# Three ends of layers rewritten: the last two steps by token half, the root table loaded ahead, shorter norms, and the projection in four PSUM bank pairs

## What is computed

```
def rms_norm(x, g):
    y = xf * rsqrt(mean(xf * xf, axis=-1) + 1e-6);  return y * g

mix  = token_mixer(rms_norm(h, g_mix_pre), ...)          # ends in y @ w_out      "out2"
h    = h + rms_norm(mix, g_mix_post)
ff   = conv_ffn(rms_norm(h, g_ffn_pre), ...)             # w_up: "ffn2", w_down: "down2"
h    = h + rms_norm(ff, g_ffn_post)
e    = p @ w_ple_proj                                    # 256 -> 2048            "proj"
gate = sigmoid(rms_norm(h, g_ple_in) @ w_ple_gate)       # 2048 -> 2048           "ple"
h    = h + rms_norm(e * gate, g_ple_post)                # the output
```

## Time and profile before

| | us |
|---|---|
| median of 3 runs | 2517.32 (2517.01 to 2519.24) |
| the profiled execution, its own time | 2519.18 |
| its span | 2517.4 |
| TensorE matmuls busy | 2472.1 (98%), 11947 instructions |
| VectorE busy | 1463.8 (58%), 1747 |
| ScalarE busy | 1245.5 (49%), 1596 |
| GpSimd busy | 44.9 (2%), 103 |
| mean granted clock of TensorE | 0.994 of 2.4 GHz |

### The profile page before, as it was taken

The page is one execution under the profiler, slowest core; times in us unless marked ns, Lnnn a source line. Parts: engine busy times, 40 slices in busy tenths (PEclk is TensorE's granted clock), DMA queues, the critical chain, the costliest instruction groups (busy, mean ns, idle before and its releaser), DMA issues.

```text
span 2517.4 us, 32623 instructions
## 1 busy us (share of the span) xinstructions
PE 2472.1 (98%) x11947; PEld 2065.4 (82%) x11947; DVE 1463.8 (58%) x1747; ACT 1245.5 (49%) x1596; POOL 44.9 (2%) x103
## 2 busy tenths in 40 slices
PE   8999999999999999999999999989999999999997
PEld 6888878888888888888888888878888888888876
DVE  5479665545454454446567566566666666544465
ACT  4357744444444444444654355455555565444453
POOL 2300000000000000000000000000000000000000
PEclk9999999999999999999999999999999999999999
DMA  7553445666666665555655455645656656655543
GB/s 247 175 139 112 135 146 184 189 192 190 185 191 186 190 195 200 189 192 175 170 173 144 143 151 180 192 146 175 198 178 190 183 183 190 203 192 193 194 164 133
DMA packets 234754, 446.27 MB, mean 177 GB/s; under 512 B 14288, under 2 KB 31012, under 8 KB 234144
## 3 DMA queue, kind: packets, MB, share of 16 engines
q1 hardware_dynamic: 231920, 434.83, 56.2%
q0 software_dynamic: 2736, 10.10, 1.3%
HBM read 442.78 MB, written 2.10 MB: 177 GB/s over the span
## 4 chain that ended last, share of the span: by engine, by line
PE 95%; DVE 3%; ACT 1%; issue 1%; DMA 0%; SPq 0%; DVEq 0%; ACTq 0%
PE pg L2092 27%; PE pg L2094 26%; PE pg L2093 26%; PE pg L2131 3%; PE pg L2132 3%; PE pg L2133 3%; PE pt L2707 1%; DVE wlo L1285 1%; PE pt L2547 1%; PE pt L2143 1%; PE pt L2251 1%; PE pt L2316 1%; PE pt L2342 1%; PE pt L2329 0%; DVE H L1391 0%
## 5 line engine op out<-in xcount | busy, mean ns | idle before, releaser
L1285 DVE TENSOR_TENSOR wlo<-raw,whi 128x1024 fp32r<-128x1024 f32 (+3 forms) x844 | 1005.2, 1197 | 984.9 <-ACT whi L647 983.3
L647 ACT ACTIVATE whi<-raw 128x1024 fp32r<-128x1024 f32 (+3 forms) x844 | 872.5, 1036 | 1185.7 <-PE pg L2094 1067.2
L2092 PE MATMUL pg<-whi,AH 128*128 128x512 f32 (+1 forms) x1920 | 748.5, 390 | 6.0 <-DVE AL L1402 4.4
L2094 PE MATMUL pg<-whi,AL 128*128 128x512 f32 (+1 forms) x1920 | 742.0, 386 | 0.0
L2093 PE MATMUL pg<-wlo,AH 128*128 128x512 f32 (+1 forms) x1920 | 741.4, 386 | 0.0
L2092 PEld LDWEIGHTS pg<-whi,AH 128*128 128x128 f32 x1920 | 361.4, 188 | 77.9 <-DVE AL L1402 5.3
L2094 PEld LDWEIGHTS pg<-whi,AL 128*128 128x128 f32 x1920 | 361.1, 188 | 73.4
L2093 PEld LDWEIGHTS pg<-wlo,AH 128*128 128x128 f32 x1920 | 361.6, 188 | 70.6
L2092 PE MATMUL pg<-whi,FH 128*128 128x512 f32 x704 | 274.5, 390 | 0.0
L2094 PE MATMUL pg<-whi,FL 128*128 128x512 f32 x704 | 274.0, 389 | 0.0
L2093 PE MATMUL pg<-wlo,FH 128*128 128x512 f32 x704 | 273.9, 389 | 0.0
(11 more groups left out here) (452 smaller groups left out, 2013.6 us busy)
## 6 DMA issues: line engine op xcount, KB each, us to landing
raw<-w_up SPq DMA_DIRECT2D x264, 512.0 KB, 3.8
raw<-w_down SPq DMA_DIRECT2D x176, 512.0 KB, 3.6
raw<-w_in SPq DMA_DIRECT2D x152, 512.0 KB, 3.6
raw<-w_gate SPq DMA_DIRECT2D x88, 512.0 KB, 3.6
raw<-w_out SPq DMA_DIRECT2D x64, 512.0 KB, 3.6
raw<-w_ple_gate SPq DMA_DIRECT2D x32, 512.0 KB, 3.8
raw<-w_in SPq DMA_DIRECT2D x32, 388.0 KB, 3.3
raw<-w_in SPq DMA_DIRECT2D x16, 280.0 KB, 3.0
```

Of the source, the lines that this page charges most:

```text
L647: A(whi[:, n % RING, 0:w], raw[:, n % RING, 0:w], ACT.Copy).then_inc(hi_ready, 1)
L1285: V.tensor_tensor(wlo[:, n % RING, 0:w], raw[:, n % RING, 0:w], whi[:, n % RING, 0:w].bitcast(F32), ALU.subtract).then_inc(lo_ready, 1)
L2092: mm(o, xh, wh, start=first and k == 0, stop=False)
L2094: ins = mm(o, xl, wh, start=False, stop=last and k == SK - 1)
```

## The change

1. **Last two steps by token half** (`last_two` on TensorE, in `out2`, `down2` and `ple`). Before, each of the last two steps did both halves. Now both steps' products of half 0 come first (`half_used`), then those of half 1 (`step_used` by 2). ScalarE reads half 0 while half 1 is computed.
2. **Root table ahead.** ScalarE's and VectorE's loops end two splits earlier (30 of 32, 86 of 88). `root_table` comes after them and before the last squares; the two splits left come after the root.
3. **After the sums.** VectorE takes the root's result and goes on to `H` at once; the product with the gain of the last chunk (`evac(3)`) comes later: in `out2` inside `ffn2`'s first chunk (`last_add`), in `down2` after two splits. The first quarter of `H` is added in two pieces of 256 columns (`post_first`), each turned and cut alone (`turn_part`, `prep_part`). The turns of the other quarters come at steps 1, 3 and 5.
4. **Norms.** `inverse` folds the last two small steps into one and the -0.5 into the first (5 or 6 small instructions instead of 6 or 7); for the three post-norms the first one comes before the wait for the root. The norms of `in1` and `ffn1` leave two steps between their squares and their root; in `ffn2` and `ple` ScalarE squares both halves.
5. **Projection.** Its four chunks get four pairs of banks (`e_bank`: `pg`, `pt` 0 and 1, `pt` 2 and 3, `pg`); ScalarE alone copies them out (`e_copy`). The first turn of `ple` comes before the projection's last chunk.
6. **Tail.** Gate, product and squares go by token half; `e_gained` writes to `FO` and follows each gate at once.

The core of the diff:

```
+            def last_two(n, b, kt0, hi, lo):
+                for t in range(NT):
+                    o = pg[:, b + t, :]
+                    for i in range(2):
+                        if t == 0:
+                            pe.wait_ge(lo_ready, n + i + 1)
+                        for k in range(SK):
+                            ...
+                            mm(o, xh, wh, start=False, stop=False)
+                            mm(o, xh, wl, start=False, stop=False)
+                            ins = mm(o, xl, wh, start=False, stop=i == 1 and k == SK - 1)
+                    if t == 0:
+                        ins.then_inc(half_used, 1)
+                    else:
+                        ins.then_inc(step_used, 2)

+            def e_bank(c, t):
+                b = 2 * ((G["proj"]["C"] + c) % 2)
+                return (pg[:, b + t, :], pt[:, t, :], pt[:, 2 + t, :], pg[:, b + t, :])[c]

             def rstd(i, n, before=False):
+                if i not in (5, 7, 9):
+                    dve.wait_ge(root, i + 1)
+                link(V.tensor_scalar(SM[:, 6:8], SM[:, 0:2], -0.5 / n, -0.5 * EPS, ALU.mult, ALU.add))
                 dve.wait_ge(root, i + 1)
-                link(V.tensor_scalar(SM[:, 6:8], SM[:, 0:2], 1.0 / n, EPS, ALU.mult, ALU.add))
-                refine(SM[:, 8:10], SM[:, 6:8], SM[:, 2:4], SM[:, 10:12])
-                ...
-                V.tensor_tensor(SM[:, 4:6], SM[:, 8:10], SM[:, 10:12], ALU.mult).then_inc(rstd_ready, 1)
+                inverse(SM[:, 4:6], SM[:, 6:8], SM[:, 2:4], SM[:, 8:10], SM[:, 10:12], SM[:, 4:6] if before else None)\
+                    .then_inc(rstd_ready, 1)

 VectorE, end of out2:
+            post_sums(8)
             rstd(5, D)
-            dve.wait_ge(gained, 4)
-            post_add(MIX, 0)
+            dve.wait_ge(gained, 3)
+            post_first(MIX)
+            prep_part(5, f2_cols, AH, AL, 0)
             post_add(MIX, 1)
-            f2_in(0)()
+            prep_part(5, f2_cols, AH, AL, 1)
+            split(F2["N"] + 2)
+            f2_in(1)()
+            split(F2["N"] + 3)
             post_add(MIX, 2)
-            f2_in(1)()
-            post_add(MIX, 3)
+            def last_add():
+                evac(3, 0, G["out2"]["N"] + 32)
+                dve.wait_ge(gained, 4)
+                post_add(MIX, 3)
             ffn(F2, ...
-                {1: f2_in(2), 2: f2_in(3), 4: norm_ffn2})
+                {2: f2_in(2), 3: last_add, 4: f2_in(3), 7: lambda: rstd(6, D)})

 VectorE, between down2 and ple:
-            proj(0)
+            post_sums(16)
             rstd(7, D)
+            dve.wait_ge(gained, 7)
+            split(p0["N"] + 2)
+            post_first(FO)
+            split(p0["N"] + 3)
+            evac(3, 0, G["down2"]["end"])
+            post_add(FO, 1)
+            split(g["N"])
+            prep_part(6, ple_cols, OH2, OL2, 0)
+            prep_part(6, ple_cols, OH2, OL2, 1)
+            split(g["N"] + 1)
+            post_add(FO, 2)
+            ple_in(1)()
+            split(g["N"] + 2)
             dve.wait_ge(gained, 8)
-            ...
             post_add(FO, 3)
+            split(g["N"] + 3)

 TensorE, projection and ple:
+            proj(0)
+            proj(1)
+            proj(2)
+            pe.wait_ge(e_out, 4)
+            pe.wait_ge(h_first, 2)
+            turn_part(6, 0)
+            pe.wait_ge(h_block, 5)
+            turn_part(6, 1)
+            proj(3)
```

More of the change, by code:

```diff
@@ L1201, in _ @@
             evac = evac_squares(G["out2"], 0)
-            for i in range(32):
+            for i in range(30):
                 between.get(i, no)()
@@ L1619, in side @@
                         dve.wait_ge(x_landed[c], 16)
[L1620 removed]
+                    squares(0, H[:, 1, :], XN[:, 1, :])
+                if n == 5:
+                    rstd(0, D)
                 if n == 10:
@@ L2024, in _ @@
+            for i in range(4 * S_ - 2):
+                hooks.get(i, no)()
+                split(g["N"] + RING + i)
+                if i % S_ == S_ - 1:
+                    evac(i // S_, 0, g["N"] + i + 1)
             if upto < 18: return
-            def proj(c):
-                evac_copy(E, G["proj"])(c, 0, G["proj"]["N"] + c + 1)
-                split(G["ple"]["N"] + c)
-            proj(0)
+            p0, g = G["proj"], G["ple"]
+            ple_cols = lambda k: V_GPLE + k
+            ple_in = lambda c: lambda: prep(6, ple_cols, OH2, OL2, c)
@@ L2047, in _ @@
-            ple_in(1)()
-            between = {(0, 1): ple_in(2), (0, 2): ple_in(3), (0, 4): norm_ple}
-            def e_gained(c):
-                dve.wait_ge(gain_landed, 64)
-                dve.wait_ge(sq_ready, 16 + 2 * c + 2)
-                for t in range(NT):
-                    x = E[:, t, c * CW:(c + 1) * CW]
-                    ins = V.tensor_tensor(x, x, GP[:, c * CW:(c + 1) * CW], ALU.mult)
-                ins.then_inc(gained, 1)
-            g = G["ple"]
+            dve.wait_ge(gained, 7)
@@ L2562, in f2_pair @@
                 else:
-                    first(5, h_tiles, lambda q: pe.wait_ge(h_block, q + 1), AH, AL, F2)
+                    chunk(F2, 0, before=lambda j: post_turns(5, AH, AL, 0, j, 1))
                 chunk(F2, 2 * c + 1, 0, 4, dc, dn)
@@ L2584, in down @@
                 for c in range(1, 4):
-                    chunk(g, c, hi=FH, lo=FL, before=before(c))
+                    two = g is G["down2"] and c == 3
+                    chunk(g, c, 0, g["S"] - 2 if two else g["S"], hi=FH, lo=FL, before=before(c))
+                if two:
+                    last_two(g["end"] - 2, 2 * ((g["C"] + 3) % 2), FKT - 2 * SK, FH, FL)
             def fox_q():
@@ L2800, in _ @@
             out2(2, 0, 8, 16)
-            out2(3, 0, 8, 24)
+            out2(3, 0, 6, 24)
+            last_two(G["out2"]["end"] - 2, 2 * ((G["out2"]["C"] + 3) % 2), 2 * SK, OHG, OLG)
             if upto < 17: return
```

280 lines of the change are left out of this document (196 added, 84 removed).

## The result

| us | median | executions |
|---|---|---|
| before, four executions beside it | 2517.39 | 2517.01 to 2519.24 |
| after | 2503.64 | 2502.72 to 2508.06 |
| predicted | 2500.3 | range 2496.8 to 2506.5 |

The ratio is 0.9947 (95% interval 0.993 to 0.9965): 13.8 us faster. The profiled execution of after is the slowest of its four: 2508.06, span 2506.3, mean granted clock 0.994; the others have 0.996 and 0.997.

The account below looks back on a forecast made before the run. Matmuls fill 98% of the span, so gains come only where TensorE waits or runs at its low clock. Terms 1.6 + 0.4 + 2.5 + 10.2 + 2.3 = 17.0 us gave 2500.3 us, range 2496.8 to 2506.5.

Parts of the forecast that it names:

- Start of in1: At in1's start, the 1.45 us wait for AL at 33.80 goes, with the slower first matmul: 1.6 us less.
- Start of in2: At in2's start, two waits for wlo each lose one small norm step of 0.2 us: 0.4 us less.
- End of out2: From out2's end into ffn2, a shorter chain to the first add, clock low for 6.8 us: 2.5 us less.
- down2, proj, ple: From the projection to ple's first chunk, 36 matmuls cover the norm, one 0.9 us wait, full clock: 10.2 us less.
- Rival (a): VectorE becomes the bound between down2 and ple, wait 2.5 us and clock falls: 5 us less gain, 2505.3; chance 0.17.
- Tail: Behind the last matmul, half 0's gate and squares go under matmuls, products go ahead: 2.3 us less.
- (b): out2 brings only its worst, 0.9 us, and the starts of in1 and in2 half of theirs: 2502.9; chance 0.10.
- (c): The clock stays full at out2: 2498.1; chance 0.07.
- (d): ScalarE loads the root's table again behind the half's squares, 1.3 us at out2, hidden at down2: 2501.6; chance 0.03.
- rival (e): Slower through low clock behind four short waits: 19 us lost makes it even, a fifth stretch gives 2522; chance 0.03.
- the four waits that the change makes: Short TensorE waits expected in the changed kernel: 3.1, 1.2 and 0.9 us at out2, 0.9 in ple.
- the last line of the sum: The median was put 1.9 us below the profiled execution's 2502.2, as in the kernel before: 2500.3.

Follow-up runs that it names:

- again: The changed kernel run once more with no edit, for a second profile: median 2505.74 us, ratio 0.995.
- before_again: The kernel before the change run once more, unchanged, for a second profile: median 2517.85 us.
- fill_level2: The changed kernel with five useless matmuls (1.13 us) ahead of level 2 of the HGRN sums, in TensorE's 1.41 us wait for Z: ratio 0.9942.
- in1_norm_as_before: The changed kernel with in1's norm as before, root and small steps right behind the squares: median 2503.68 us.
- fill_out2: The changed kernel with useless matmuls in TensorE's idle time behind out2, 13 ahead of ffn2's first turn and 4 behind it: median 2506.27 us.

## Why the prediction was right, step by step

Against the table, before to changed kernel:

- **Start of in1, -1.6.** "To XD" went from 338.9 to 337.2 (mean of eleven profiles with the edit): -1.7. Right, and so is the wait that went.
- **Start of in2, -0.4.** "XD to Z" without the low clock 987.1 to 986.7: -0.4. Its waits are 0.79 and 0.36 where they were 0.96 and 0.57.
- **End of out2, -2.5.** 752.9 to 750.0 in the first profile, 750.3 to 751.3 in the other five that leave this stretch alone, -1.5 to -2.9. The prediction's own terms add up to 2.6. First turn after 3.17 (3.1 predicted), waits 1.0 (1.2) and 0.66 (0.9), half adds 0.42 (0.40). The clock was low for 6.8 us (6.8), but that hit is partly luck: the term was read from one stretch of 6.8 us behind another wait, and it measured 10.2 us in `again`.
- **down2, proj, ple, -10.2.** 112.6 to 102.5, -10.1, against the second profile of before -8.7. The one wait is 0.65 (0.9). The eight transposes come without a wait, no chunk's end waits, the clock is full. Rival (a) is out. But "the clock falls as it did behind 2.6", its price, is no rule: in `before_again` the clock stayed full behind the same wait.
- **Tail, -2.3.** 15.5 to 13.2 (the four terms add up to 2.4), with the table load on the path (2494.22, 1.28 us) and the eight adds of 5.39 us as in the earlier trace rows.

Rivals (b), (c) and (d) are out for the same reasons: `out2` brought 1.5 at least, the clock was low there, and no second load came. The times alone could not tell: (b) stands at 2502.9 and (a) at 2505.3, on both sides of the first median, 2503.64, and beside the second, 2505.74. The stretches do.

The five terms sum to 17.0, and the same stretches of the profiles to 14.6 at the least and 17.4 at the most. The median gave 13.8, then 12.1. So the time lies in the range, but two steps between the sum and the time were wrong, and both concern the low clock.

The first is the one by which I dismissed rival (e): "1.45 us at 33.80 left the clock alone". I looked for new low stretches behind the four waits that the change makes, and there the sum's one at `out2` is all there is. Another came behind a wait that the change doesn't touch but moves: the one for `Z` ended 2.4 us earlier in `again` than in the kernel before, and 1.1 later in after, where 3.2 us had been lost at 337. It cost 3.2 us in both profiles of the changed kernel, and the one at 337 another 3.2 in one of them. Against the predicted span of 2500.4, `again` has 2504.2 (3.2 for `Z`, the rest mostly at `out2`) and after 2506.3 (twice 3.2, less 0.5). `fill_level2`, with neither of the two, has 2500.4, the predicted span. It and `in1_norm_as_before` show the stretch at `Z` from two sides, by filling the wait and by moving it.

The second is the last line of the sum: "the same difference gives 2500.3". The 1.9 us between the profiled execution and the median were taken over from the kernel before. There `before_again`'s profile, 1.7 us shorter at 2517.46, shows what most of it was: one low stretch less behind `down2`, 1.4 us. Behind `down2` the changed kernel has no low stretch, so no run shows such a difference in it; four of the executions of `fill_level2` lie at 2502.3 to 2502.5, where the prediction had 2502.2 for the profiled one.

Of the 3.3 us between 2500.3 and 2503.64, up to 1.9 are thus this step and the rest low stretches, which by the mean clocks came in some executions and not in others. How often, and at which moments, stays open. The mechanism was right in each place; that the median came within 3.3 us of the forecast and not 5.4, as `again`'s did, is luck.

## What to carry to other kernels

Where matmuls fill 98% of the span, put work that needs no result under the serial end of a layer: 24 matmuls in spare banks were worth 7 us here, 4.85 of waiting and 2.3 of low clock. Count as the price of a wait of TensorE not only its length but the low clock that may follow, 3.2 us behind 1.4, and expect that a gain early in the program moves every later wait to another moment. A wait that left the clock alone in one profile, or made it fall, is no proof for the next. So compare stretches between fixed instructions of the two traces, not the totals. Where TensorE must idle for 1 us or more, a few matmuls into a bank that is free anyway kept the clock full at two places here (`fill_level2`, `fill_out2`), in the profiles; with one place filled the median need not follow, since other short waits are left.

## What the runs showed of the hardware

- The granted clock fell (from 2.4 to 1.2 GHz) behind waits of 0.82 and 1.41 us in some profiles and not in others, with the same instructions in front and behind. With the wait of 1.41 us moved by 1.3 us (one profile) it stayed full, and so it did with 1.13 us of the wait filled with matmuls (two profiles).
- Nor does a longer wait always bring it: it fell around the 2.60 us wait for `E` in one profile of the kernel before and stayed at 1.0 in the other.
- It did not fall at once: in `again` the wait ended at 1323.69 with the clock at 1.0, and the fall came at 1325.4, among the narrow matmuls. It then stayed at half for 6.8 us, though TensorE was busy throughout.
- A table load of ScalarE may start while VectorE computes what the next root needs, so that only 1.08 of its 1.28 us were late.
